# The head of a layer in a streaming encoder step: key latents projected last and normalised when their products are read out

## The chip, the cores and the metric

The kernel runs on one core of a Trainium2 chip. The metric is the device time of one execution in microseconds (us). Three timed runs of the kernel before took 2825.91, 2833.0 and 2838.61 us (median 2833.0). Two changed kernels that differ by less than about half a per cent (14 us) can hardly be told apart at that spread.

## The reference, cut to what matters

The program computes two layers for 576 tokens at once: 512 of a prompt and 64 of a sample that also sees 256 cached tokens. Each layer begins with one norm and one wide projection, of which the first three groups of columns concern us:

```python
u = rms_norm(x, g_pre_mix)                       # 576 x 1024
zq, zkv, zpe, ... = split_cols(u @ w_in)         # 384, 256, 32 columns, ...
q_a = rms_norm(zq, g_mla_q) @ w_mla_uq           # per head: 64 plain + 32 rotary columns
q_nope, q_pe = q_a[..., :64], rope(q_a[..., 64:], pos)
ckv = rms_norm(zkv, g_mla_kv)                    # key latents, also an output
kpe = rope(zpe, pos)                             # rotary key, shared by the heads, also an output
kv = concat([cache_ckv, ckv]) @ w_mla_ukv        # per head: 64 key + 64 value columns
o_a = softmax(q . k * scale, masked) @ v         # 8 heads
```

Then follow retention, band attention, the merge of the three branches, cross-attention and the MLP, and the same again in the second layer. Everything is float32.

## The kernel before, in words

All activations are held feature-major: 128 features lie on the partitions, 576 tokens along the free axis. Weights come as "units" of 128x1024; ACT starts the DMA of a unit, copies it into a rounded high part (`hi`), and POOL subtracts that from the raw unit to give the low part (`lo`, one instruction of 128x1024 on SBUF). A product is the sum of three matmuls (high by high, high by low, low by high), so an activation must be split in the same way before TensorE can take it.

A `project` is one "job": for kt tiles of 128 input features, 6 matmuls each (three products, two halves of 288 tokens), into one of two job buffers in PSUM. DVE reads each job out ("evicts" it) and so frees its buffer; TensorE waits in `slot()` until the buffer of the job before last is free. A job from the 1024-wide input has 48 matmuls; a job of one head from the key latents has 12, the one for the 256 cached tokens 6 (narrower), the query job 18.

An RMS norm's sum of squares is made by TensorE too: ACT squares a tile (`square`), and TensorE multiplies it with a matrix of ones (`stat`, 4 matmuls). ACT then takes the square root (`root_of`), and DVE the reciprocal (`invert`).

Order at the head of a layer (lines 431 to 436 on TensorE, 760 to 776 on ACT, 1094 to 1119 on DVE): the two jobs of the key latents (`CKV`), the job of the rotary key, two stats of the key latents, the three jobs of the query latents (`ZQ`). DVE evicts each job times the reciprocal of the input norm (`scale_job`), rotates the rotary key (1102 to 1106), inverts the key norm (1107), multiplies both key latents by gain and norm in place (1110), and splits key latents and cached latents in one piece of 1664 columns (1114). ACT rounds the three query latents and DVE makes their low parts (1119).

Then the first head begins (`steps_mla(0)` and the entry -1 of `PLAN_MLA`, where a plan says after which attention tile a step of the next head is issued, and -1 means ahead of the first): key/value job of the new tokens and of the cached ones, the three stats of the query latents, the query job, the transposition of the values (`turn_values`), and the two key/value jobs of the second head. DVE at that place evicts keys and values (1144 to 1148), inverts the query norm (1127), multiplies the rotary tables `COS` and `SIN` by it (1128, 1129), copies four rows of mask from `COS` into both query buffers (1131), and evicts the queries (1134 to 1139). Only then come the scores of the first tile. The query norm thus enters through the tables, and the key norm is already inside `CKV`. Each engine runs its own list in order, and all waits are on semaphores.

The lines that the change and the steps below touch:

```python
1110    v.scalar_tensor_tensor(out=CKV[:, k, 0:NT], in0=CKV[:, k, 0:NT], scalar=g_col("mla_kv", k),
1127    invert(rstd2[:, :])
1128    v.tensor_tensor(COS[0:QK, :], COS[0:QK, :], rstd2[0:QK, :], ALU.mult)
1129    v.tensor_tensor(SIN[QK:P, :], SIN[QK:P, :], rstd2[QK:P, :], ALU.mult)
1131    v.tensor_copy(Q[QK:QK + MASKS, c], COS[QK:QK + MASKS, :])
1145    free(v.tensor_copy(halves(vT[:, 0:NT]), job_halves(s)))
```

Of the kernel before, what the change touches and what calls it, by code (L numbers as in the profile page):

```python
# [13 lines left out]
P = 128  # L14
# [87 lines left out]
PLAN_MLA = plan(MLA_HEADS, NQ, (-1, 0, 2))  # L102
# [12 lines left out]
READY = 42  # L115
ROUNDS = 33
# [10 lines left out]
def build(nc, x_in, mem_in, w_in, ckv_in, kpe_in, state_in, bandk_in, bandv_in, memk_in, memv_in,  # L127
          bias_in, gain_in, gain_x_in, const_in, rope_in, mask_in, y_out, ckv_out, kpe_out, retp_out, rets_out,
          bandk_out, bandv_out, memk_out, memv_out):
    with ExitStack() as ctx:  # L130
# [42 lines left out]
        rstd_c = TMP[:, 1]  # L173
# [79 lines left out]
        def _(pe):  # L253
# [15 lines left out]
            with pe.Fori(0, DEPTH) as l:  # L269
# [45 lines left out]
                def project(s, kt, hl, at_col=0, step=P, m=P, pieces=HALVES, each_ready=0, stats=False,  # L315
                            each_evicted=False):
# [5 lines left out]
                    for k in range(kt):  # L322
                        if stats:
                            stat(k, kt)
                        if each_ready and k % each_ready == 0:
                            wait_ready()
# [104 lines left out]
                for i in range(CR + 1):  # L431
                    project(unit(), KT, U_HL, each_ready=int(i == 0))
                for k in range(CR):
                    stat(k, CR)
                for i in range(QR):
                    project(unit(), KT, U_HL)

                def steps_mla(h):
                    s = []

                    def keys_values():
                        if h == 0:
                            wait_ready()
                        s.append(unit())
                        project(s[0], CR, CKV_HL, at_col=QR * P)
                        project(s[0], CR, CKV_HL, at_col=QR * P, pieces=[(0, PAST, NT)])

                    def queries():
                        if h == 0:
                            for k in range(QR):  # L450
                                stat(k, QR)
                            wait_ready()
                        project(s[0], QR, ZQ_HL)

                    return [keys_values, queries,
                            lambda: turn_values(V_TOKENS + [(NT, P, 4), (NT + P, P, 5), (SEQ, DEC, 6)], but=1)]
# [147 lines left out]
        def _(act):  # L604
# [40 lines left out]
            with act.Fori(0, DEPTH) as l:  # L645
# [114 lines left out]
                for _ in range(CR + 1):  # L760
                    place()
                    n["job"] += 1
                for k in range(CR):
                    act.wait_ge(job_free, l * JOBS + k + 1 + 2)
                    square(k, CKV[:, k, 0:NT])
                root_of(rstd_c, CR * P)
                for _ in range(QR):
                    place()
                    n["job"] += 1
                evicted()  # L770
                for k in range(QR):
                    ins = round_hi(ZQ_HL[0][:, k], ZQ[:, k], "mla_q", k)
                ins.then_inc(rounded, 1)
                for k in range(QR):
                    square(k, ZQ[:, k])
                root_of(rstd2[:, :], QR * P)
# [8 lines left out]
                def steps_mla(h):  # L785
                    return [count(2, 1), count(1), count(1)]
# [103 lines left out]
        def _(dve):  # L890
# [19 lines left out]
            with dve.Fori(0, DEPTH) as l:  # L910
# [183 lines left out]
                for k in range(CR):  # L1094
                    scale_job(CKV[:, k, 0:NT])
# [11 lines left out]
                invert(rstd_c)  # L1107
                scale_job(ZQ[:, 1])
                for k in range(CR):
                    v.scalar_tensor_tensor(out=CKV[:, k, 0:NT], in0=CKV[:, k, 0:NT], scalar=g_col("mla_kv", k),  # L1110
                                           in1=rstd_c, op0=ALU.mult, op1=ALU.mult)
                dve.drain()
                z = Z0 + 2 * QR * NT
                is_ready(split(m_sb[:, QR * NT:QR * NT + CR * KEYS], arena[:, z:z + CR * KEYS],
                               arena[:, z + CR * KEYS:z + 2 * CR * KEYS]))
                scale_job(ZQ[:, 2])
                store()
                store()
# [578 lines left out]
```

## Time and profile before

| what | value |
|---|---|
| median of three timed runs | 2833.0 us |
| the profiled execution, its own time | 2829.17 us |
| its span in the trace | 2827.4 us |
| mean granted clock of TensorE | 0.959 of full |
| TensorE busy (matmul) | 2606.2 us, 92% |
| VectorE (DVE) busy | 1443.0 us, 51% |
| ScalarE (ACT) busy | 799.8 us, 28% |
| GpSimd (POOL) busy | 826.7 us, 29% |
| shares of the chain that ended last | PE 79%, DVE 10%, DVEq 6%, issue 2%, ACT 1% |

Busy times are sums over the whole span, and what bounds one stretch is seen only there. The chain that ended last goes back from the last instruction to what released it at each step; DVEq is the time in which DVE's own queue, its drains above all, passed from one instruction to the next. The granted clock is a share of TensorE's full 2.4 GHz; 0.5 is its lower level, 1.2 GHz. Where rows have a start time, it counts from the start of the span; the head of the first layer lies at 20 to 87 us, that of the second at 1411 to 1481 us, 1393.45 us later.

### The profile page before, as it was taken

To read this page: it belongs to the slowest core of one execution; us is meant where nothing else is said; L and a number is where in the kernel's file an instruction comes from. 1 tells how busy PE (TensorE), PEld (TensorE's weight loads), DVE (VectorE), ACT (ScalarE), POOL (GpSimd) and SP (SyncE) were. 2 spreads that over 40 slices of the span, in tenths; PEclk is the share of its full clock that TensorE was granted. 3 is DMA by queue.
4 is the path that set the end of the run, shared out by engine and by line. 5 is a ranking of instruction groups with operands and counts; after the bars stand their busy time and mean duration, and the time that the engine had idled before them with its cause. 6 is when DMAs were issued, how large, how long until landed. Compare 5 with 4: busy or idle time off the path is not lost.

```text
span 2827.4 us, 46601 instructions
## 1 busy us (share of the span) xinstructions
PE 2606.2 (92%) x17836; PEld 2395.7 (85%) x17836; DVE 1443.0 (51%) x2226; ACT 799.8 (28%) x1460; POOL 826.7 (29%) x335
## 2 busy tenths in 40 slices
PE   8789999999989799999788999899999898999996
PEld 7669888877988799999676798797779787999995
DVE  4661464354564755346756515624445648353366
ACT  4342112234324311111324421223343343111112
POOL 3113223211333234434221132132223232343342
PEclk9999999999999999999899999899999999999998
DMA  4102112221223122222221121121222221222222
GB/s 140 38 23 93 60 47 85 71 75 61 83 71 94 46 82 84 88 82 84 61 82 31 48 83 49 43 92 61 81 76 80 68 89 48 83 85 83 82 83 78
DMA packets 65687, 204.73 MB, mean 72 GB/s; under 512 B 7936, under 2 KB 16000, under 8 KB 65360
## 3 DMA queue, kind: packets, MB, share of 16 engines
q10 hardware_dynamic: 47808, 174.08, 20.1%
q1 hardware_dynamic: 17680, 27.90, 3.0%
q8 instruction: 136, 2.23, 0.3%
q14 instruction: 63, 0.52, 0.1%
HBM read 190.93 MB, written 11.03 MB: 71 GB/s over the span
## 4 chain that ended last, share of the span: by engine, by line
PE 79%; DVE 10%; DVEq 6%; issue 2%; ACT 1%; DMA 0%; SPq 0%; ACTq 0%
PE job L332 65%; PE outp L381 5%; PE scores L360 3%; DVE rstd L974 3%; PE turn L370 2%; DVEq L1001 2%; PE scores L262 1%; DVEq L1037 1%; PE job L341 1%; DVE arena L965 1%; DVE rstd L982 1%; PE job L350 1%; ACT probT L705 1%; DVE x L1002 1%; DVEq L980 0%
## 5 line engine op out<-in xcount | busy, mean ns | idle before, releaser
L332 PE MATMUL job<-arena,w_hi 128*128 128x288 f32 (+1 forms) x9984 | 1775.5, 300 | 46.5 <-DVE q L1139 16.7
L332 PEld LDWEIGHTS job<-arena,w_hi 128*128 128x128 f32 x9984 | 1494.3, 192 | 67.6 <-issue 22.3
L593 POOL TENSOR_TENSOR w_lo<-raw,w_hi 128x1024 fp32r<-128x1024 f32 x331 | 826.5, 2497 | 1968.7 <-ACT w_hi L612 1968.7
L332 PE MATMUL job<-arena,w_lo 128*128 128x288 f32 (+1 forms) x4992 | 1087.6, 297 | 0.0
L332 PEld LDWEIGHTS job<-arena,w_lo 128*128 128x128 f32 x4992 | 818.8, 191 | 0.0
L612 ACT ACTIVATE w_hi<-raw 128x1024 fp32r<-128x1024 f32 x331 | 349.6, 1056 | 1072.0 <-PE job L332 904.7
L381 PEld LDWEIGHTS outp<-probT,v 128*64 128x64 f32 (+2 forms) x992 | 111.4, 149 | 141.5 <-issue 71.3
L948 DVE TENSOR_TENSOR tmp<-job,rstd 128x576 f32<-128x576 f32 x70 | 53.0, 758 | 329.9 <-PE job L332 325.5
L381 PE MATMUL outp<-probT,v 128*64 128x128 f32 (+2 forms) x992 | 160.8, 291 | 51.4 <-DVE arena L1045 38.7
L262 PE MATMUL scores<-q,const 128*128 128x288 f32 (+1 forms) x296 | 99.0, 473 | 69.6 <-ACT q L673 60.6
L360 PE MATMUL scores<-k,q 128*128 128x256 f32 (+10 forms) x400 | 148.5, 455 | 13.1 <-DVE k L1341 4.4
L937 DVE CAST arena<-tmp 128x576 fp32r<-128x576 f32 x64 | 151.6, 2368 | 4.7
L716 ACT ACTIVATE arena<-outp 64x128 fp32r<-64x128 f32 (+3 forms) x200 | 52.4, 262 | 312.9 <-PE outp L381 312.5
L262 PEld LDWEIGHTS scores<-q,const 128*128 128x128 f32 x296 | 60.8, 222 | 92.1 <-ACT q L673 69.2
L1387 DVE TENSOR_TENSOR m<-job,m 128x576 f32<-128x576 f32 x48 | 36.4, 758 | 194.3 <-PE job L332 194.3
L747 ACT ACTIVATE tmp<-tmp,gain 128x576 f32<-128x576 f32 x48 | 37.3, 778 | 256.4 <-DVE tmp L948 256.4
L1376 DVE SCALAR_TENSOR_TENSOR tmp<-job,rstd 128x576 f32<-128x576 f32 x64 | 48.5, 758 | 110.4 <-PE job L332 110.1
L943 DVE COPY m<-job 128x576 f32<-128x576 f32 x48 | 36.3, 756 | 124.9 <-PE job L332 124.9
L370 PE MATMUL turn<-const,prob 128*128 128x128 f32 (+1 forms) x496 | 99.7, 300 | 0.0
L974 DVE RECIPROCAL rstd<-rstd 128x576 f32<-128x576 f32 x22 | 82.5, 3752 | 31.3 <-ACT rstd L626 27.4
L705 ACT ACTIVATE probT<-turn 128x256 f32<-128x256 f32 (+3 forms) x200 | 83.6, 418 | 36.4 <-PE turn L370 32.3
L1045 DVE TENSOR_TENSOR arena<-outp,arena 64x128 fp32r<-64x128 f32 (+3 forms) x200 | 55.0, 275 | 65.3 <-ACT arena L716 60.8
(145 smaller groups left out, 1718.1 us busy)
## 6 DMA issues: line engine op xcount, KB each, us to landing
raw<-in_w ACTq DMA_DIRECT2D x332, 512.0 KB, 3.6
bias<-in_bias SPq DMA_DIRECT2D x16, 256.0 KB, 3.4
x<-in_x SPq DMA_DIRECT2D x4, 576.0 KB, 8.7
cs<-in_rope SPq DMA_DIRECT2D x4, 576.0 KB, 4.6
out_o_bandk<-k SPq DMA_DIRECT2D x8, 288.0 KB, 4.0
out_o_bandv<-tmp SPq DMA_DIRECT2D x8, 288.0 KB, 5.0
out_y<-x SPq DMA_DIRECT2D x1, 2304.0 KB, 6.9
bias<-in_mem SPq DMA_DIRECT2D x8, 256.0 KB, 3.5
```

The lines of the kernel that those rows point to most:

```text
L262: mm = pe.matmul(scores_ps[:, po:po + nn], ONES, SQ[:, k % 2, so:so + nn], start=(k == 0), stop=(k == kt - 1))
L332: mm = pe.matmul(ps[0:m, po:po + nn], w[:, s, c:c + m], x[:, k, so:so + nn], start=(k == 0 and w is WHI and x is hl[0]), stop=(k == kt - 1 ...
L360: pe.matmul(score_ps[s][:, 0:w], Q[r0:r1, head["q"], t0:t0 + P], K[r0:r1, head["k"], c:c + w], start=True, stop=True).then_inc(score_done, 1)
L370: mm = pe.transpose(turn_ps[0:w, j * P:(j + 1) * P], PROB[:, it % 3, c:c + w], IDENT)
L381: mm = pe.matmul(out_ps[o0:o0 + v1 - v0, 0:P], V[0:w, head["vs"], t, v0:v1], probT[0:w, j * P:(j + 1) * P], start=(j == 0), stop=(j == len ...
L593: nc.gpsimd.tensor_tensor(WLO[:, u % RING, :], RAWS[:, u % RAW, :], WHI[:, u % RING, :].bitcast(F32), ALU.subtract).then_inc(lo_done, 1)
L612: act.activation(WHI[:, u % RING, :], RAWS[:, u % RAW, :], ACT.Copy).then_inc(hi_done, 1)
L705: ins = act.activation(probT[:, 0:full * P], turn_ps[:, 0:full * P], ACT.Copy)
L937: v.tensor_copy(hi, src)
L974: v.reciprocal(ap, ap)
L1001: dve.drain()
L1045: v.tensor_tensor(O_HL[1][o0:o1, ot, t0:t1], out_ps[o0:o1, c0:P], O_HL[0][o0:o1, ot, t0:t1].bitcast(F32), ALU.subtract).then_inc(out_free, 1)
```

## The change

Three things change in the head of each layer, and nothing else.

First, the order of the jobs: rotary key, three query latents, two key latents. The stats stand in the middle of the jobs (after four of the eight input tiles): those of the first two query latents inside the third query job, the third inside the first key job, that of the first key latent inside the second key job, and that of the second key latent ahead of the first query job. ACT rounds, squares and takes the root of each latent as it is evicted (`latent`). DVE now splits the cached latents alone (512 columns, between the evictions of the second and third query latent), makes the low parts of the queries, inverts the query norm and multiplies both tables, and then evicts the two key latents.

Second, the key norm. The key latents are multiplied by their gain alone on the way into the split (by ACT and DVE, as the query latents are). The reciprocal of the norm is multiplied where a head's key and value job is evicted: the two copies become multiplications by `rstd_c`, which now lies in `rstd2`, and it is inverted at the first head's eviction, behind the queries. The latents that are an output get gain and norm in place later, ahead of the value eviction of the second head (`store_latents`).

Third, the steps of a head: the first head runs cached keys and values, queries, new keys and values, and then its transposition, which waits for all evictions (`but=0`); the others run new, cached, queries, values. `PLAN_MLA` has four steps in place of three, the first two at the same tile.

```diff
-PLAN_MLA = plan(MLA_HEADS, NQ, (-1, 0, 2))
+PLAN_MLA = plan(MLA_HEADS, NQ, (-1, -1, 0, 2))
...
-rstd_c = TMP[:, 1]
+rstd_c = rstd2
...
             for k in range(kt):
                 if stats:
                     stat(k, kt)
+                if amid and k == kt // 2:
+                    amid()
                 if each_ready and k % each_ready == 0:
...
-        for i in range(CR + 1):
-            project(unit(), KT, U_HL, each_ready=int(i == 0))
-        for k in range(CR):
-            stat(k, CR)
-        for i in range(QR):
-            project(unit(), KT, U_HL)
+        def latent_stats(*which):
+            def add():
+                for k, kt in which:
+                    stat(k, kt)
+            return add
+        project(unit(), KT, U_HL, each_ready=1)
+        for after in (None, None, latent_stats((0, QR), (1, QR)), latent_stats((2, QR)), latent_stats((0, CR))):
+            project(unit(), KT, U_HL, amid=after)
         def steps_mla(h):
             s = []
-            def keys_values():
+            def weights():
+                if not s:
+                    s.append(unit())
+                return s[0]
+            def past():
                 if h == 0:
                     wait_ready()
-                s.append(unit())
-                project(s[0], CR, CKV_HL, at_col=QR * P)
-                project(s[0], CR, CKV_HL, at_col=QR * P, pieces=[(0, PAST, NT)])
+                project(weights(), CR, CKV_HL, at_col=QR * P, pieces=[(0, PAST, NT)])
             def queries():
                 if h == 0:
-                    for k in range(QR):
-                        stat(k, QR)
+                    stat(CR - 1, CR)
                     wait_ready()
-                project(s[0], QR, ZQ_HL)
-            return [keys_values, queries,
-                    lambda: turn_values(V_TOKENS + [(NT, P, 4), (NT + P, P, 5), (SEQ, DEC, 6)], but=1)]
+                project(weights(), QR, ZQ_HL)
+            def new():
+                if h == 0:
+                    wait_ready()
+                project(weights(), CR, CKV_HL, at_col=QR * P)
+            first = [past, queries, new] if h == 0 else [new, past, queries]
+            return first + [
...
-        for _ in range(CR + 1):
+        def latent(i):
+            act.wait_ge(job_free, l * JOBS + i + 2 + 2)
+            k, kt = (i, QR) if i < QR else (i - QR, CR)
+            src, hi_of, name = (ZQ[:, k], ZQ_HL[0][:, k], "mla_q") if i < QR else \
+                (CKV[:, k, 0:NT], CKV_HL[0][:, k, 0:NT], "mla_kv")
+            if i == 0:
+                act.wait_ge(layer_loaded, (l + 1) * 16 * LAYER_LOADS)
+            ins = round_hi(hi_of, src, name, k)
+            if k == kt - 1:
+                ins.then_inc(rounded, 1)
+            square(k, src)
+            if k == kt - 1:
+                root_of((rstd2 if i < QR else rstd_c)[:, :], kt * P)
+        for i in range(1 + QR + CR):
             place()
+            if i >= 2:
+                latent(i - 2)
             n["job"] += 1
-        for k in range(CR):
-            act.wait_ge(job_free, l * JOBS + k + 1 + 2)
-            square(k, CKV[:, k, 0:NT])
-        root_of(rstd_c, CR * P)
-        for _ in range(QR):
-            place()
-            n["job"] += 1
-        evicted()
-        for k in range(QR):
-            ins = round_hi(ZQ_HL[0][:, k], ZQ[:, k], "mla_q", k)
-        ins.then_inc(rounded, 1)
-        for k in range(QR):
-            square(k, ZQ[:, k])
-        root_of(rstd2[:, :], QR * P)
+        latent(QR + CR - 1)
...
-            return [count(2, 1), count(1), count(1)]
+            return [count(1, 1), count(1), count(1), count(1)]
...
-        for k in range(CR):
-            scale_job(CKV[:, k, 0:NT])
         scale_job(TMP[:, 0])
         scale_job(ZQ[:, 0])
@@ -1104,33 +1120,35 @@
         dve.drain()
         for b in range(2):
             v.tensor_tensor(K[NOPE:QK, b, 0:NT], TMP[NOPE:QK, 0], RTMP[NOPE:QK, :], ALU.add)
-        invert(rstd_c)
         scale_job(ZQ[:, 1])
+        is_ready(split(CKV[:, :, NT:KEYS], CKV_HL[0][:, :, NT:KEYS], CKV_HL[1][:, :, NT:KEYS]))
+        scale_job(ZQ[:, 2])
+        is_ready(lows(lambda k: ZQ[:, k], "mla_q", ZQ_HL, 0, QR))
+        invert(rstd2[:, :])
+        v.tensor_tensor(COS[0:QK, :], COS[0:QK, :], rstd2[0:QK, :], ALU.mult)
+        v.tensor_tensor(SIN[QK:P, :], SIN[QK:P, :], rstd2[QK:P, :], ALU.mult)
         for k in range(CR):
-            v.scalar_tensor_tensor(out=CKV[:, k, 0:NT], in0=CKV[:, k, 0:NT], scalar=g_col("mla_kv", k),
-                                   in1=rstd_c, op0=ALU.mult, op1=ALU.mult)
+            scale_job(CKV[:, k, 0:NT])
         dve.drain()
-        z = Z0 + 2 * QR * NT
-        is_ready(split(m_sb[:, QR * NT:QR * NT + CR * KEYS], arena[:, z:z + CR * KEYS],
-                       arena[:, z + CR * KEYS:z + 2 * CR * KEYS]))
-        scale_job(ZQ[:, 2])
-        store()
-        store()
-        is_ready(lows(lambda k: ZQ[:, k], "mla_q", ZQ_HL, 0, QR))
+        is_ready(lows(lambda k: CKV[:, k, 0:NT], "mla_kv", tuple(t[:, :, 0:NT] for t in CKV_HL), 0, CR))
+        def store_latents():
+            for k in range(CR):
+                v.scalar_tensor_tensor(out=CKV[:, k, 0:NT], in0=CKV[:, k, 0:NT], scalar=g_col("mla_kv", k),
+                                       in1=rstd_c[:, :], op0=ALU.mult, op1=ALU.mult)
+            store()
+            store()
         def steps_mla(h):
             b = h % 2
             def queries():
+                s = job()
                 if h == 0:
-                    invert(rstd2[:, :])
-                    v.tensor_tensor(COS[0:QK, :], COS[0:QK, :], rstd2[0:QK, :], ALU.mult)
-                    v.tensor_tensor(SIN[QK:P, :], SIN[QK:P, :], rstd2[QK:P, :], ALU.mult)
                     for c in range(2):
                         v.tensor_copy(Q[QK:QK + MASKS, c], COS[QK:QK + MASKS, :])
-                    dve.drain()
-                s = job()
                 v.scalar_tensor_tensor(out=halves(Q[0:QK, b]), in0=job_halves(s, 0, QK), scalar=QK ** -0.5,
                                        in1=halves(COS[0:QK, :]), op0=ALU.mult, op1=ALU.mult)
                 v.scalar_tensor_tensor(out=halves(RTMP[NOPE:QK, :]), in0=job_halves(s, QK, P), scalar=QK ** -0.5,
@@ -1138,22 +1156,31 @@
                 dve.drain()
                 free(v.tensor_tensor(Q[NOPE:QK, b], Q[NOPE:QK, b], RTMP[NOPE:QK, :], ALU.add))
-            def keys_values():
+            def new_keys_values():
                 s = job()
-                v.tensor_copy(halves(K[0:NOPE, b, 0:NT]), job_halves(s, 0, NOPE))
-                free(v.tensor_copy(halves(vT[:, 0:NT]), job_halves(s)))
+                if h == 0:
+                    invert(rstd_c[:, :])
+                v.tensor_tensor(halves(K[0:NOPE, b, 0:NT]), job_halves(s, 0, NOPE), halves(rstd_c[0:NOPE, :]),
+                                ALU.mult)
+                free(v.tensor_tensor(halves(vT[:, 0:NT]), job_halves(s), halves(rstd_c[:, :]), ALU.mult))
+            def past_keys_values():
                 s = job()
                 v.tensor_copy(K[0:NOPE, b, NT:KEYS], job_ps[s][0:NOPE, 0:PAST])
                 free(v.tensor_copy(vT[:, NT:KEYS], job_ps[s][:, 0:PAST]))
             def values():
+                if h == 1:
+                    store_latents()
                 s = job()
                 v.tensor_copy(V[:, b, 0:4, 0:MLA_V], tiles(job_ps[s][:, 0:512], 4)[:, :, NOPE:P])
                 v.tensor_copy(V[:, b, 4:6, 0:MLA_V], tiles(job_ps[s][:, 512:768], 2)[:, :, NOPE:P])
                 free(v.tensor_copy(V[0:DEC, b, 6, 0:MLA_V], job_ps[s][0:DEC, 768 + NOPE:768 + P]))
-            return [keys_values, queries, values]
+            steps = [new_keys_values, past_keys_values, queries, values]
+            return [steps[i] for i in (1, 2, 0, 3)] if h == 0 else steps
...
-for i in range(CR):
-    add(cols(zkv + i * P))
 pe_w = w[:, zpe:zpe + ROPE]
 add(w_tile(np.concatenate([np.zeros((D, NOPE), np.float32), pe_w, swapped(pe_w)], 1)))
 for i in range(QR):
     add(cols(zq + i * P))
+for i in range(CR):
+    add(cols(zkv + i * P))
```

## Rows read from the trace of the kernel before

**Rows 1.** Windows: stretch, length; busy PE, PEld, DVE, ACT, POOL; granted clock; DMA.

```profile
1422.00:1454.00 32.00, 32.00 (x235) 31.46 (x233) 13.75 (x12) 6.02 (x7) 11.74 (x5) 1.00 0.26 81
1454.00:1476.00 22.00, 10.96 (x58) 9.63 (x58) 18.29 (x21) 7.96 (x10) 4.86 (x2) 0.82 0.25 79
82.00:98.00 16.00, 13.12 (x61) 10.53 (x61) 8.72 (x22) 3.87 (x13) 0.00 (x0) 0.78 0.00 0
```

**Rows 2.** Timeline by start, second layer: TensorE's first instructions after its gaps.

```profile
1456.76 0.79 PE L332 MATMUL job<-arena,w_hi 128*128 128x288 f32 x4 [2.65 <-DVE arena L939]
1475.42 1.33 PE L332 MATMUL job<-arena,w_hi 128*128 128x288 f32 x4 [8.38 <-DVE q L1139]
1480.80 0.92 PE L360 MATMUL scores<-k,q 100*128 100x128 f32 x4 [1.53 <-DVE tmp L1148]
```

**Rows 3.** Timeline, first layer: the first scores.

```profile
86.79 0.92 PE L360 MATMUL scores<-k,q 100*128 100x128 f32 x4 [1.00 <-DVE tmp L1148]
```

**Rows 4.** Chain that ended last, second layer: start, length, piece.

```profile
1464.69 3.75 DVE rstd L974
```

**Rows 5.** Timeline, second layer, while the projections run.

```profile
1426.63 0.76 DVE L948 TENSOR_TENSOR m<-job,rstd 128x576 f32<-128x576 f32 x1 [5.64 <-PE job L332]
1427.59 1.24 ACT L673 ACTIVATE q<-m 128x576 f32<-128x576 f32 x2
1427.77 2.41 POOL L593 TENSOR_TENSOR w_lo<-raw,w_hi 128x1024 fp32r<-128x1024 f32 x1 [3.93 <-ACT w_hi L612]
1432.83 2.10 PE L262 MATMUL scores<-q,const 128*128 128x288 f32 x8
1434.55 0.91 PE L332 MATMUL job<-arena,w_hi 128*128 128x288 f32 x4
```

**Rows 6.** Timeline, second layer: POOL beside DVE on SBUF.

```profile
1468.53 0.75 DVE L1128 TENSOR_TENSOR cs<-cs,rstd 96x576 f32<-96x576 f32 x1
1468.97 2.51 POOL L593 TENSOR_TENSOR w_lo<-raw,w_hi 128x1024 fp32r<-128x1024 f32 x1 [0.95 <-ACT w_hi L612]
1469.30 2.80 DVE L1129 TENSOR_TENSOR cs<-cs,rstd 32x576 f32<-32x576 f32 x1
```

**Rows 7.** Forms of lines 937, 1131: ns min/median/max, first and last start.

```profile
L937 DVE CAST arena<-tmp x64: 459/2495/2499, 988.6 to 2735.6; 128x576 fp32r<-128x576 f32 x64
L1131 DVE COPY q<-cs x4: 449/449/450, 77.9 to 1472.4; 4x576 f32<-4x576 f32 x4
```

**Rows 8.** Timeline, second layer: rounding, stats and queries of the first head.

```profile
1457.21 2.11 ACT L629 ACTIVATE arena<-m,gain 128x576 fp32r<-128x576 f32 x3 [8.32 <-DVE m L948]
1463.50 0.91 PE L332 MATMUL job<-arena,w_hi 128*128 128x288 f32 x4
1463.91 0.74 ACT L626 ACTIVATE rstd<-scores,const 128x576 f32<-128x576 f32 x1 [1.33 <-PE scores L262]
1465.67 2.35 POOL L593 TENSOR_TENSOR w_lo<-raw,w_hi 128x1024 fp32r<-128x1024 f32 x1 [14.32 <-ACT w_hi L612]
1466.11 0.93 PE L350 MATMUL job<-const,tmp 128*128 128x128 f32 x7
1473.01 0.76 DVE L1134 SCALAR_TENSOR_TENSOR q<-job,cs 96x576 f32<-96x576 f32 x1 [0.17 <-issue]
1478.59 0.75 DVE L1144 COPY k<-job 64x576 f32<-64x576 f32 x1 [2.45 <-PE job L332]
```

**Rows 9.** A window behind the second layer's first gap.

```profile
1458.00:1462.00 4.00, 4.00 (x17) 3.56 (x17) 2.65 (x4) 2.57 (x5) 0.00 (x0) 0.60 0.48 168
```

**Rows 10.** Costliest groups: the weights' high part on ACT: busy, mean ns, idle.

```profile
L612 ACT ACTIVATE w_hi<-raw 128x1024 fp32r<-128x1024 f32 x331 | 349.6, 1056 | 1072.0 <-PE job L332 904.7
```

**Rows 11.** Form of line 1110; timeline at the second head's values, first layer.

```profile
L1110 DVE SCALAR_TENSOR_TENSOR m<-m,gain,tmp x4: 810/812/815, 58.5 to 1452.6; 128x576 f32<-128x576 f32 x4
...
99.89 0.28 DVE L1045 TENSOR_TENSOR arena<-outp,arena 64x128 fp32r<-64x128 f32 x1 [0.38 <-ACT arena L716]
100.83 1.09 PE L381 MATMUL outp<-probT,v 128*64 128x128 f32 x8 [0.25 <-ACT probT L705]
```

More of the change, by code:

```diff
@@ L114 @@
 REQS = 3 * KT + RET_HEADS + RET_HEADS // 2
-READY = 42
-ROUNDS = 33
+READY = 43
+ROUNDS = 34
 ROOTS = 9 + RET_HEADS
@@ L315, in project @@
                 def project(s, kt, hl, at_col=0, step=P, m=P, pieces=HALVES, each_ready=0, stats=False,
-                            each_evicted=False):
+                            each_evicted=False, amid=None):
                     ps = slot()
@@ L458, in _ @@
+                    return first + [
+                            lambda: turn_values(V_TOKENS + [(NT, P, 4), (NT + P, P, 5), (SEQ, DEC, 6)], but=min(h, 1))]
                 heads = [dict(q=h % 2, k=h % 2, rows=(0, QK + MASKS), tiles=Q_TILES, vs=h % 2,
```

## The prediction

> **What bounds the kernel now.** I read the stages by windows first. While the projections of a layer's head run, TensorE is busy for 32.00 of 32 us at full clock; right behind them it is busy for only 10.96 of 22 us and DVE for 18.29 [rows 1]. So only that short stretch, once a layer, can change much. The timeline shows its gaps: 2.65 us until DVE has split the key latents, 8.38 us until it has evicted the first queries, and 1.53 us until the evictions ahead of the first scores [rows 2]. In the first layer the first scores start at 86.79, which is 1480.24 on the second layer's time [rows 3]; in the second at 1480.80 [rows 2]. The chain that ended last runs through the query norm's reciprocal, 3.75 us from 1464.69 [rows 4]. What counts is thus when DVE is through with the evictions that the first scores need, not TensorE's busy share.
>
> **Up to the fifth job.** I work on the second layer's time; the first layer has the same steps. The third job has been issued at 1432.83 and a job takes 6.40 us (evictions of 0.76 with 5.64 of waiting for TensorE between them); two stats take 1.72, until 1434.55 [rows 5]. The new order moves no matmul off TensorE: the same six jobs and five stats run. The fourth job, with two stats inside, ends at 1432.83 + 6.40 + 1.72 = 1440.95; ACT has squared the first two latents by about 1435.5, before they are wanted at 1436.03. The fifth, with one stat, ends at 1448.21. The split of the cached latents (512 of 1664 columns) and the rotation of the key lie on DVE between evictions 6.40 us apart and cost nothing; without that cover the split costs under the 2.65 us that the whole one shows [rows 2].
>
> **The sixth job, a new wait.** It wants the square of the first key latent at its middle, 1448.21 + 3.20 = 1451.41. DVE evicts that latent only behind the query norm and both tables. The third query latent is evicted by 1441.9; ACT first rounds a weight unit, 1.06 us from about 1441.1 [rows 10], then the latent, until 1442.9; then DVE makes three low parts. POOL starts 1.34 us behind a job's issue end (1427.77, the job before the eviction at 1426.63 having ended at 1426.43) and runs 2.4 us [rows 5]. The product of two SBUF tiles on 32 partitions that starts 0.33 us after POOL takes 2.80 us and ends 0.62 after POOL does, where its neighbour took 0.75 [rows 6]. So the first low part waits for POOL until 1444.6, all three are done at about 1446.75, the reciprocal of 3.75 [rows 4] at 1450.5; then the table product meets POOL's next unit (1449.55 to 1451.95) and ends at 1452.55, the second table at 1453.2, the eviction at 1454.05. ACT starts 0.2 behind it, rounds in 0.70 (three in 2.11 [rows 8]) and squares in 0.7: stat at 1455.65. TensorE waits 4.25 us. Bounds: 2.5 if neither meeting happens; 6.4 if POOL's weight unit comes late and holds the second table too. I take 4.25, since both meetings follow from job ends. The job's end is then 1455.65 + 0.86 + 3.20 = 1459.7; before, all six were through at 1434.55 + 3 x 6.40 = 1453.75.
>
> **From there to the first scores.** Eviction of the second key latent to 1460.65, ACT as above, last stat at 1462.25, issued by 1463.1 (call it S). The cached keys' job fits in between. Queries 2.61 us (1463.50 to 1466.11 [rows 8]), visible to DVE at S + 2.8. ACT's root starts at S + 0.41 and POOL's next unit at S + 2.17, as before (1463.50, 1463.91, 1465.67 [rows 8]), so POOL is 0.6 us ahead of the two mask copies. Alone such a copy takes 0.449 us; a cast of SBUF to SBUF takes 0.459 alone and 2.495 in most of its 64 runs [rows 7]. No row shows the copy beside POOL, so its bounds are 0.82 us for both and S + 2.17 + 2.35 + 0.75 = S + 5.3 for their end; I take the latter, since the cast is the nearest row. Query eviction 2.4 (1473.01 [rows 8] to 1475.42, where TensorE is released [rows 2]) with a drain: S + 7.85. Now the key norm's reciprocal, 3.75, which nothing covers: S + 11.75. Two products of 0.76 out of PSUM, 1.5: S + 13.3 = 1476.4. TensorE waits for this with the transposition (`but=0`), behind which the second head's two jobs stand: a gap of about 9 us, in place of the 8.38. Before, from the queries' release (1475.42) to the first scores it took 5.38 [rows 2]; now the transposition, 0.95, stands ahead of the same two jobs: 1476.4 + 0.95 + 5.38 = 1482.75. Bounds: 1.4 less if those jobs run at full clock (4 matmuls from 1475.42 took 1.33, 0.91 at most elsewhere [rows 2, 5]; twelve at 6.40 us per 48 are 1.6, and DVE's first eviction, now at 1478.59 [rows 8], comes 1.4 earlier), 1.0 more if the transposition too runs at half clock.
>
> Against before: 1482.75 - 1480.80 = +1.95 in the second layer and 1482.75 - 1480.24 = +2.5 in the first. **Head: +4.45.** The two removed gaps come back as two others.
>
> The Trainium skill, SBUF — State Buffer, section Who interferes with whom, says that an fp32 copy from SBUF to SBUF takes the port pair that DVE shares with GpSimd and is blocked for a whole GpSimd instruction. By it the copies wait as I have them; without it the copies end at S + 3.6, and the sum would be 3.4 us lower in all, 2834.1. No run here shows this form beside POOL; the cast of rows 7 agrees with the page.
>
> **Gain and norm of the stored latents.** They leave the path at the head, where they took two instructions of 0.812 us, and stand ahead of the second head's value eviction [rows 11]. Behind that on DVE are the maxima of the sixth tile and the release of an output, which ends at 100.17 now and at 101.8 then; TensorE's next weighting starts at 100.83 and needs it [rows 11]. So about 0.95 of the 1.65 us comes through per layer, bounds 0 and 1.8 (a drain more): **+1.9.** The two output DMAs asked for behind it start later on SP, which has nothing else to issue until the eight heads are done, and only there DVE waits for them.
>
> **Evictions of keys and values.** Copies of 0.75 us [rows 8] become products of 0.76 [rows 5] out of PSUM: two in each of 16 heads, 0.3 us if none is hidden, nothing where TensorE is the bound. I take 0. The plan's fourth step changes no order beyond the first head.
>
> **The clock.** TensorE's clock fell to 0.60 in the 4 us behind a gap of 2.65 us [rows 9]; the new gap of 4.25 stands inside a job whose second half, 3.20 us, is all on the path. At half clock for that half: +3.2; not at all: 0. I take 1.0 a layer, nearer to none, as only a part of the half need lie in such a stretch: **+2.0.**
>
> **Sum.** 4.45 + 1.9 + 2.0 = +8.35 us: 2829.17 + 8.35 = 2837.5. The profiled execution lies 3.8 us under the median of the timed runs (2833.0) and inside their spread; I state 2838, a little on the median's side of the sum.
>
> **Rivals.** (1) The meetings with POOL don't happen and the clock holds: the sixth job waits 1.75 less, the copies cost 1.7 less, the jobs at the end 1.4 less, and 1.0 of clock falls away: -5.85 a layer, 2837.5 - 11.7 = 2826. For it: the meetings hang on half microseconds. Against it: POOL's starts are tied to the same job ends as DVE's work.
> (2) The change wins what it takes away: the query norm is off the path and nothing takes its place, both gaps of 2.65 and 8.38 go: -22, 2807. For it: the query norm now has two jobs beside it. Against it: the key norm's reciprocal stands in the same place of DVE's list.
> (3) Slower: the clock. With gaps of 4.25, about 2 and 9 us within 27 us, TensorE stays at 1.2 GHz from the sixth job's middle well into the first head. Price a layer: second half +3.2, last stat and queries +3.5, transposition +1, and in the attention +2 (82 to 98 us had a mean of 0.78 in the first layer [rows 1]), less the 1.0 counted: +8.7, 2837.5 + 17.4 = 2855. It decides from a clock at 0.5 throughout 1455 to 1466. Against it: even behind the gap of 8.38 us that mean is well over 0.5, so the clock comes back soon after work does.
>
> **How the numbers follow.** Forecast 0.68, rival 1 0.15, rival 2 0.06, rival 3 0.11. Under 0.5% (14 us) a run cannot be told from no change; forecast and rival 1 lie within that, though 0.01 of the forecast's end is slower: faster 0.06, same 0.82, slower 0.12. The bounds give, per layer, -5.85 and -0.95 (stores hidden) against +2.1 (a longer sixth wait), +2.2 (clock), +0.85 and +1: 2824 to 2850. That leaves out rivals 2 and 3, 0.17.
>
> **What would show it.** In the changed trace: TensorE's wait inside the sixth job for ACT's square, 2.5 to 6; the table product lengthened by POOL; mask copies of over 2 us; the reciprocal behind the query eviction with TensorE idle for 7 to 10 us ahead of the transposition; first scores 1 to 4 us later from the head's start than before. I am wrong if DVE evicts the first key latent before 1452, or if the gap ahead of the transposition is under 5 us.

## The result, and the profile after

The changed kernel takes 2840.59 us (median of 20 runs, 2820.70 to 2845.62), the kernel before 2830.48 beside it (20 runs, 2812.15 to 2839.36). The ratio is 1.0035 with an interval of 1.002 to 1.005: slower, by 5.7 to 14.2 us; the middle of that, 9.9, lies under the half per cent (14 us) that was taken as hard to tell from no change. The forecast was 2838, its sum +8.35. The ratio of the version with both mends, further down, leaves out one execution of 2944.83 us, whose mean granted clock was 0.83 where the others had 0.96.

One measure serves for all that follows. "Head" is the time from the start of DVE's eviction of the third job to the start of the first scores; first layer, then second:

| kernel | head, us | against before |
|---|---|---|
| before | 47.21, 47.77 | |
| after | 51.88, 52.03 | +4.67, +4.26 |

The evictions at which it starts in the second layer, before and after; the first scores are in [rows 2], [rows 3] and further down:

```profile
1433.03 0.76 DVE L948 TENSOR_TENSOR tmp<-job,rstd 128x576 f32<-128x576 f32 x1 [5.64 <-PE job L332]
...
1437.21 0.76 DVE L966 TENSOR_TENSOR m<-job,rstd 128x576 f32<-128x576 f32 x1 [0.43 <-PE job L334]
```

The windows of the second layer in the changed kernel (stretch, length; busy PE, PEld, DVE, ACT, POOL; granted clock; DMA share and GB/s) answer to [rows 1]:

```profile
1422.00:1454.00 32.00, 32.00 (x232) 31.37 (x232) 15.80 (x14) 9.76 (x12) 10.38 (x4) 1.00 0.24 78
1456.00:1460.00 4.00, 0.04 (x1) 0.00 (x0) 2.61 (x3) 1.33 (x2) 0.48 (x1) 0.83 0.02 9
1460.00:1465.00 5.00, 4.93 (x16) 4.36 (x17) 0.00 (x0) 0.02 (x1) 0.00 (x0) 0.50 0.00 0
1465.00:1468.00 3.00, 2.69 (x19) 2.48 (x18) 0.76 (x1) 0.19 (x1) 0.00 (x0) 0.92 0.00 0
1483.00:1486.00 3.00, 2.90 (x13) 2.87 (x14) 0.74 (x3) 1.03 (x1) 0.00 (x0) 0.51 0.00 0
```

While the projections run, nothing differs for TensorE. Then it stands still for 4 us; it starts again at 0.50, which is 1.2 of 2.4 GHz, and has its full clock back only after 1465. The timeline names the wait (start, length, engine, line; in brackets the idle time before and what ended it):

```profile
1447.29 3.85 DVE L983 SCALAR_TENSOR_TENSOR arena<-m,gain,arena 128x576 fp32r<-128x576 f32 x3 [1.00 <-ACT arena L643]
1451.06 3.74 DVE L992 RECIPROCAL rstd<-rstd 128x576 f32<-128x576 f32 x1
1454.11 2.37 POOL L607 TENSOR_TENSOR w_lo<-raw,w_hi 128x1024 fp32r<-128x1024 f32 x1 [5.04 <-ACT w_hi L626]
1454.87 2.22 DVE L1128 TENSOR_TENSOR cs<-cs,rstd 96x576 f32<-96x576 f32 x1
1457.88 0.76 DVE L966 TENSOR_TENSOR m<-job,rstd 128x576 f32<-128x576 f32 x1
1460.07 2.29 PE L262 MATMUL scores<-q,const 128*128 128x288 f32 x4 [4.02 <-ACT q L687]
1461.74 1.57 PE L334 MATMUL job<-arena,w_hi 128*128 128x288 f32 x4
1466.82 0.40 PE L334 MATMUL job<-arena,w_hi 128*128 128x256 f32 x2
...
1472.25 2.38 POOL L607 TENSOR_TENSOR w_lo<-raw,w_hi 128x1024 fp32r<-128x1024 f32 x1 [15.77 <-ACT w_hi L626]
1472.86 2.46 DVE L1151 COPY q<-cs 4x576 f32<-4x576 f32 x2 [2.04 <-PE job L334]
1477.73 3.75 DVE L992 RECIPROCAL rstd<-rstd 128x576 f32<-128x576 f32 x1
1483.10 1.75 PE L352 MATMUL job<-const,tmp 128*128 128x128 f32 x7 [8.67 <-DVE tmp L1166]
1484.50 1.31 PE L334 MATMUL job<-arena,w_hi 128*128 128x288 f32 x4
1489.24 0.92 PE L362 MATMUL scores<-k,q 100*128 100x128 f32 x4 [1.54 <-DVE tmp L1172]
```

Read down DVE: low parts (L983), the query norm's reciprocal (L992), a table product (L1128) that ends behind POOL, and only then the eviction of the first key latent (L966), whose square TensorE awaits inside the sixth job: 4.02 us. A second such chain ends in 8.67 us of waiting ahead of the transposition: mask copies (L1151) that end behind POOL, the queries' evictions, and the key norm's reciprocal, uncovered. The gaps of 2.65 and 8.38 us [rows 2] are gone, and these stand in their place. A smaller wait, 1.51 us, stands ahead of the last stat. The first layer has the same two long ones, 4.02 and 8.68.

The stored latents, first layer, at the second head's values:

```profile
101.56 0.62 PE L383 MATMUL outp<-probT,v 128*64 128x128 f32 x4 [1.44 <-DVE arena L1063]
103.35 1.54 DVE L1138 SCALAR_TENSOR_TENSOR m<-m,gain,rstd 128x576 f32<-128x576 f32 x2
106.04 0.27 DVE L1063 TENSOR_TENSOR arena<-outp,arena 64x128 fp32r<-64x128 f32 x1
106.46 1.06 PE L383 MATMUL outp<-probT,v 128*64 128x128 f32 x8 [0.99 <-DVE arena L1063]
```

From the weighting of four matmuls to that of eight it now takes 106.46 - 101.56 = 4.90 us, 4.16 before. The release of an output (L1063) ends the wait, as [rows 11] let expect.

The sum of the traces is 4.67 + 4.26 + 2 x 0.75 = +10.4 us, inside the measured 5.7 to 14.2. The two profiled executions themselves differ by 3.2 us of span, so about 7 us the other way lie outside these places, 6.0 of them behind the second layer's first scores; single executions of one kernel differ by more than that (2812.15 to 2839.36 before), and I did not trace the cause.

### The profile page after: what moved, and what is told of

It reads as the page before. It is cut to its first block, busy times and chain, and to the rows that moved or that the text cites. A ratio compares the mean times of both kernels' runs of the same rounds, so it can differ in the third digit from the quotient of the medians.

```text
span 2830.6 us, 46613 instructions
## 1 busy us (share of the span) xinstructions
PE 2605.2 (92%) x17836; PEld 2393.1 (85%) x17836; DVE 1447.0 (51%) x2230; ACT 802.9 (28%) x1464; POOL 827.7 (29%) x335
## 4 chain that ended last, share of the span: by engine, by line
PE 79%; DVE 10%; DVEq 6%; issue 3%; ACT 1%; DMA 0%; ACTq 0%; SPq 0%
PE job L334 65%; PE outp L383 4%; PE scores L362 3%; DVE rstd L992 2%; PE turn L372 2%; DVEq L1019 2%; PE scores L262 2%; DVEq L1055 1%; DVE arena L983 1%; PE job L343 1%; DVEq L993 1%; DVE rstd L1000 1%; PE job L352 1%; ACT probT L719 1%; DVE x L1020 1%
## 5 line engine op out<-in xcount | busy, mean ns | idle before, releaser
L966 DVE TENSOR_TENSOR tmp<-job,rstd 128x576 f32<-128x576 f32 x70 | 53.1, 758 | 330.8 <-PE job L334 326.1
L992 DVE RECIPROCAL rstd<-rstd 128x576 f32<-128x576 f32 x24 | 90.0, 3750 | 29.8 <-ACT rstd L640 25.9
L362 PEld LDWEIGHTS scores<-k,q 100*128 100x128 f32 (+2 forms) x400 | 61.7, 192 | 29.8 <-issue 14.9
```

The lines of the kernel that those rows point to most:

```text
L362: pe.matmul(score_ps[s][:, 0:w], Q[r0:r1, head["q"], t0:t0 + P], K[r0:r1, head["k"], c:c + w], start=True, stop=True).then_inc(score_done, 1)
L966: free(v.tensor_tensor(halves(dst), job_halves(s), halves(rstd[:, :]), ALU.mult))
L992: v.reciprocal(ap, ap)
```

## The experiments

Theory: the change loses by its two new waits, the first with a low clock behind it. Each edit is on the changed kernel, save where said; where the verdict is a single run, it rests on the trace.

**Both key stats behind the sixth job.** The order of all else stays.

```diff
-latent_stats((2, QR)), latent_stats((0, CR))):
+latent_stats((2, QR)), None):
     ...
-stat(CR - 1, CR)
+for k in range(CR): stat(k, CR)
```

> The stat of the first key latent no longer stands inside the sixth job but with the other one, ahead of the first query job. I call 'head' the time from the start of the third job's eviction to the start of the first scores: 47.21 and 47.77 us in the two layers before, 51.88 and 52.03 after. Theory (the wait inside the sixth job holds back the eviction of the second key latent, and all that follows): the sixth job ends about 6 us earlier (4.0 us of wait, 0.9 to 1.9 us of low clock, 0.86 of stat), the last stat is issued 6 to 7.5 us earlier, the head falls to 44.5 to 46 us, and the whole kernel comes out at 0.996 to 1.000 of the time before. Rival (DVE's list sets the end, and TensorE's wait only moves to the stats ahead of the queries): the head falls by less than 2 us and the ratio stays at 1.002 to 1.005.

Heads 45.04 and 45.04; ratio to before 0.9988 (0.9965 to 1.0011, 12 runs). The first layer:

```profile
61.89 0.76 DVE L967 TENSOR_TENSOR m<-job,rstd 128x576 f32<-128x576 f32 x1 [0.64 <-PE job L334]
62.69 1.24 PE L262 MATMUL scores<-q,const 128*128 128x288 f32 x4
64.08 1.24 PE L262 MATMUL scores<-q,const 128*128 128x288 f32 x4 [0.16 <-ACT q L688]
64.94 0.90 PE L334 MATMUL job<-arena,w_hi 128*128 128x288 f32 x4
84.85 0.92 PE L362 MATMUL scores<-k,q 100*128 100x128 f32 x4 [1.41 <-DVE tmp L1173]
```

TensorE finishes the sixth job while DVE catches up, and both stats follow with 0.16 us of waiting, where the changed kernel waits 1.51 ahead of the last one. The place of one stat cost the changed kernel 6.8 to 7.0 us a layer; that alone turns its loss into no measurable difference.

**The key norm's reciprocal ahead of the query eviction**, where DVE waits for the queries' job anyway.

```diff
 def queries():
+    if h == 0: invert(rstd_c[:, :])
     s = job()
     ...
 def new_keys_values():
-    if h == 0: invert(rstd_c[:, :])
```

> The reciprocal of the key norm stands ahead of the first queries' eviction on DVE, where DVE waited 2.04 us for the query job, and no longer behind it. Theory (the reciprocal of 3.75 us is uncovered, and the mask copies are slow because POOL holds the port): the reciprocal runs from about 0.1 us behind ACT's root, the copies then come behind POOL's unit and take 0.8 us for both in place of 2.46, and the first head's key and value eviction ends 3.1 us earlier: heads of 48.8 and 48.9 us, ratio about 1.0013. Rival (the copies are slow by themselves, on 4 partitions behind a table product): they stay at 2.4 us and the heads fall by 1.5 us only, to 50.4 and 50.5.

Heads 48.52 and 48.71; ratio 1.0011 (0.999 to 1.0031). The first layer:

```profile
72.58 3.75 DVE L992 RECIPROCAL rstd<-rstd 128x576 f32<-128x576 f32 x1 [0.44 <-ACT rstd L640]
73.57 2.39 POOL L607 TENSOR_TENSOR w_lo<-raw,w_hi 128x1024 fp32r<-128x1024 f32 x1 [14.69 <-ACT w_hi L626]
76.48 0.83 DVE L1153 COPY q<-cs 4x576 f32<-4x576 f32 x2 [0.15 <-issue]
81.25 1.75 PE L352 MATMUL job<-const,tmp 128*128 128x128 f32 x7 [5.51 <-DVE tmp L1166]
```

The reciprocal lies over POOL's instruction and keeps its 3.75 us; the copies behind it take 0.83. The gap falls by 3.17 us.

**POOL's weight unit placed later** in the first head, nothing else moved.

```diff
-[count(1, 1), count(1), count(1), count(1)]
+[count(1, int(h > 0)), count(1), count(1), count(1, int(h == 0))]
```

> ACT rounds the weight unit of the first head one job later, behind the first head's new keys, so that POOL's low part does not run beside the first queries' eviction; nothing else is changed. Theory (POOL's instruction blocks the two mask copies): the copies take 0.8 us for both in place of 2.46, and the heads fall by 1.65 us to 50.2 and 50.4. Rival (they are slow for another reason): still 2.4 us, the heads as after, 51.9 and 52.0.

Heads 49.55 and 49.91, one run of 2835.98 us.

```profile
74.64 0.83 DVE L1151 COPY q<-cs 4x576 f32<-4x576 f32 x2 [2.04 <-PE job L334]
77.38 2.67 POOL L607 TENSOR_TENSOR w_lo<-raw,w_hi 128x1024 fp32r<-128x1024 f32 x1 [18.10 <-ACT w_hi L626]
```

With POOL at 77.38 instead of 73.91 the same copies take 0.83 us in place of 2.47. That is 1.64 us; the head gained 2.33 and 2.12, 0.5 to 0.65 more than expected. In the first layer 0.57 of that lies behind the new keys' eviction (6.44 us to the first scores, 7.01 in the changed kernel), in the same instructions at another clock. In the second, the stat and the rest of the sixth job took 0.90 less than in the changed kernel and the way behind the new keys' eviction 0.38 more (6.65 us for 6.27).

**Stored latents without their norm.** It leaves out the two products of `store_latents`, so the stored latents lack gain and norm.

```diff
 def store_latents():
-    for k in range(CR):
-        v.scalar_tensor_tensor(out=CKV[:, k, 0:NT], ...)
```

> Leaves out the two multiplications of the stored key latents by gain and norm ahead of the second head's value eviction (the latents given out are not normalised then); the two output DMAs stay. Theory (about half of the 1.6 us comes through): from the first scores to the fourth weighting with 8 matmuls it takes 14.0 us, as before, in place of 14.8, the heads themselves are unchanged, and nothing of the whole time can be told. Rival (wholly hidden): 14.8 still.

One run of 2844.31 us, which says nothing at this size. The measure I had named, from the first scores on, holds differences of clock too (14.04 and 12.49 us in the two layers of before), so it failed. Between the two weightings it is plain:

```profile
100.36 0.62 PE L383 MATMUL outp<-probT,v 128*64 128x128 f32 x4 [1.44 <-DVE arena L1063]
104.52 1.09 PE L383 MATMUL outp<-probT,v 128*64 128x128 f32 x8 [0.25 <-ACT probT L719]
```

4.16 us, as before, and the wait is ACT's 0.25 again [rows 11]. So the store costs 4.90 - 4.16 = 0.74 us in this layer; from the first scores to the same weighting the changed kernel takes 0.78 and 0.75 longer than the one before in the two layers.

**Matmuls on constants in the sixth job's gap**, to tell the low clock from the wait.

```diff
 def add():
+    if which == ((0, CR),):
+        for _ in range(4):
+            pe.matmul(turn_ps[:, 0:512], ONES, const[:, 0:512], ...)
```

> Four matmuls of constants (128x512, some 0.85 us each, into a bank that nothing else uses there) stand in the sixth job ahead of the wait for the stat, so that TensorE works through most of the 4.0 us gap. Theory (the second half of the sixth job ran longer, 4.2 and 5.1 us in place of 3.2, because the granted clock fell behind the gap): it takes 3.2 us in both layers, and the heads fall by 1.0 and 1.9 us, to about 50.9 and 50.1. Rival (the longer half has another cause, such as weights or reads that come late): it stays at 4.2 to 5.1 and the heads don't fall.

Heads 50.30 and 50.00, one run of 2839.63 us. The first layer; the columns of the window further down are as above:

```profile
57.83 3.59 PE L438 MATMUL turn<-const 128*128 128x512 f32 x8
62.02 1.24 PE L262 MATMUL scores<-q,const 128*128 128x288 f32 x4 [0.59 <-ACT q L690]
62.88 0.90 PE L334 MATMUL job<-arena,w_hi 128*128 128x288 f32 x4
66.28 0.40 PE L334 MATMUL job<-arena,w_hi 128*128 128x256 f32 x2
```

The half job in the second layer:

```profile
1470.50 0.89 PE L334 MATMUL job<-arena,w_hi 128*128 128x288 f32 x4
...
1473.89 0.40 PE L334 MATMUL job<-arena,w_hi 128*128 128x256 f32 x2
```

The window behind the gap, first layer:

```profile
62.00:66.00 4.00, 3.98 (x26) 3.77 (x27) 0.00 (x0) 0.00 (x0) 0.00 (x0) 1.00 0.02 4
```

The four constants (eight records) end 0.59 us ahead of the square, which comes no earlier for them; behind it the clock is 1.00. The stat takes 62.88 - 62.02 = 0.86 us instead of 1.67, and the second half of the job, to the first matmul of 256 columns, 66.28 - 62.88 = 3.40 (1473.89 - 1470.50 = 3.39 in the second layer) instead of 4.18 (first) and 1466.82 - 1461.74 = 5.08 (second). The low clock cost 0.81 + 0.78 = 1.6 us here in the first layer and 0.81 + 1.69 = 2.5 in the second. The heads fell by 1.58 and 2.03; in the second layer 0.46 went into a slower way behind the new keys' eviction (6.73 us for 6.27).

**Both mends together**, the first two edits in one kernel.

> Both mends together: the stat of the first key latent out of the sixth job, and the reciprocal of the key norm ahead of the first queries' eviction. Theory (two waits in a row on one path, so their prices add): heads of 45.04 - 3.3 = 41.7 us in both layers (47.21 and 47.77 before), ratio to before about 0.9965. Rival (with the first wait gone, the reciprocal is covered by something else that is then late, the query job or POOL's unit): heads of 43.5 to 45 us, ratio 0.998.

Heads 41.80 and 41.87; median 2819.01 us of five runs, ratio 0.9936 (0.9911 to 0.9961).

```profile
65.96 3.75 DVE L993 RECIPROCAL rstd<-rstd 128x576 f32<-128x576 f32 x1 [0.44 <-ACT rstd L641]
69.86 0.83 DVE L1154 COPY q<-cs 4x576 f32<-4x576 f32 x2
74.63 1.75 PE L352 MATMUL job<-const,tmp 128*128 128x128 f32 x7 [5.52 <-DVE tmp L1167]
81.44 0.92 PE L362 MATMUL scores<-k,q 100*128 100x128 f32 x4 [1.54 <-DVE tmp L1173]
```

The two waits were independent: the single gains would give 51.88 - 6.84 - 3.36 = 41.68 in the first layer. TensorE still waits 5.52 us ahead of the transposition.

**New keys ahead of the queries**, on top of the first mend, with the reciprocal at the new keys' eviction.

```diff
-first = [past, queries, new] if h == 0 else [new, past, queries]
+first = [past, new, queries] if h == 0 else [new, past, queries]
     ...
-turn_values(..., but=min(h, 1))
+turn_values(..., but=1)
```

> As the first mend, and the first head runs cached, new, queries, values: the two stats, the key and value job and its eviction with the reciprocal stand ahead of the queries, so that the transposition runs while DVE evicts the queries (it waits for all but the last eviction). Theory (the transposition and its gap were on the path only behind the queries): heads of 39 to 40.5 us, ratio about 0.995, better than both kernels. Rival (the first scores need the queries too, and DVE has the same list to work off, so the order inside the list is worth little against the reciprocal moved forward alone): heads of 41.5 us, as with both mends.

Heads 41.34 and 43.43; ratio 0.9951 (0.9932 to 0.997). The heads missed the theory's 39 to 40.5, though the ratio came out as it said: the first layer is where its rival put it, the second 1.6 us above both mends. The second layer:

```profile
1470.57 0.96 PE L352 MATMUL job<-const,tmp 128*128 128x128 f32 x7 [3.13 <-DVE tmp L1166]
1472.78 2.34 POOL L607 TENSOR_TENSOR w_lo<-raw,w_hi 128x1024 fp32r<-128x1024 f32 x1 [5.23 <-ACT w_hi L626]
1472.90 2.83 DVE L1157 TENSOR_TENSOR q<-q,bias 32x576 f32<-32x576 f32 x1
1475.78 1.33 PE L334 MATMUL job<-arena,w_hi 128*128 128x288 f32 x4 [4.25 <-DVE q L1157]
```

The transposition still waits 3.13 us for the eviction of the values (5.52 with both mends), and behind it the next head's key job waits again, 1.41 us in the first layer and 4.25 in the second, since it needs the buffer that only the query eviction frees. The earlier transposition also lets ACT and POOL start the next weight unit sooner, and in the second layer it meets that eviction's last add: 2.83 us in place of 0.75. In the first layer the add started 0.65 us ahead of POOL and kept 0.75.

**Constants in both gaps** (the edit above, and nine such matmuls ahead of the transposition).

> As the run with constants in the sixth job, and nine more such matmuls, some 7.7 us, behind the first head's key job, in the gap of 8.7 us ahead of the transposition. Theory (clock): the transposition takes 0.93 us in place of 1.40 from its start to the next job's, the twelve matmuls behind it 1.6 in place of 2.3 to 3.0, and the heads fall to 48.5 to 49.5 us. Rival (the evictions on DVE set the end there whatever the clock): under 0.7 us less than the run with the first filling alone.

Heads 48.24 and 48.25, one run of 2833.65 us: 2.06 and 1.75 us less than with the first gap alone filled, where the rival allowed 0.7. The transposition runs at full clock, 0.98 us against 1.75:

```profile
82.58 0.98 PE L352 MATMUL job<-const,tmp 128*128 128x128 f32 x7 [0.96 <-DVE tmp L1172]
87.40 0.92 PE L362 MATMUL scores<-k,q 100*128 100x128 f32 x4 [1.53 <-DVE tmp L1178]
```

**Both mends and six constants in the gap that they leave.**

```diff
 def new():
     ...
+    if h == 0:
+        for _ in range(6):
+            pe.matmul(turn_ps[:, 0:512], ONES, const[:, 0:512], ...)
```

> Both mends, and six matmuls of constants (some 5.1 us) behind the first head's key job, in the gap of 5.5 us that is left ahead of the transposition. Theory (the clock that falls in that gap costs the transposition 0.45 us and the second head's jobs 1.3, and the first items of the attention run slow behind it): heads of 39.8 to 40.2 us in place of 41.8, and some 2 us more inside the first head, ratio to before 0.990 to 0.993. Rival (the evictions on DVE follow at their own pace): heads of 41.3 us or more, ratio as with both mends alone (0.9936).

Heads 39.83 and 39.81; median 2816.22 us, ratio 0.9928 (0.9906 to 0.9951). This version beats the kernel before, and so do the two mends without the constants; the times of these two cannot be told apart, their heads can:

```profile
74.18 0.98 PE L352 MATMUL job<-const,tmp 128*128 128x128 f32 x7 [0.36 <-DVE tmp L1170]
79.00 0.92 PE L362 MATMUL scores<-k,q 100*128 100x128 f32 x4 [1.53 <-DVE tmp L1176]
```

The further 2 us expected inside the first head came in the first layer alone: from the first scores to the weighting of four matmuls it takes 8.33 us in place of 11.11 with the two mends, at a clock of 1.00 in place of 0.69. In the second layer it takes 9.90 and 9.91.

**Constants in the kernel before**, nine in its gap of 8.38 us.

```diff
 def values():
     turn_values(..., but=1)
+    if h == 0:
+        for _ in range(9):
+            pe.matmul(turn_ps[:, 0:512], ONES, const[:, 0:512], ...)
```

> The kernel before, with nine matmuls of constants (some 7.7 us) behind the first transposition, in its gap of 8.38 us. It tells how much of what the filling brings does not belong to the change at all. Theory (clock): heads of 45.8 and 46.3 us in place of 47.21 and 47.77, ratio 0.998 to 0.999. Rival: no change of the heads beyond 0.3 us.

Heads 45.82 and 46.20; ratio 0.9971 (0.995 to 0.9991).

```profile
80.90 0.79 PE L332 MATMUL job<-arena,w_hi 128*128 128x288 f32 x4 [0.59 <-DVE q L1144]
85.01 0.92 PE L360 MATMUL scores<-k,q 100*128 100x128 f32 x4 [1.53 <-DVE tmp L1153]
```

The matmuls that took 1.33 us behind the gap [rows 2] take 0.79, and from the first scores to the weighting of four the first layer takes 8.33 us in place of 9.88. So with the long gaps filled in both orders (the gap of 2.65 us of the kernel before was left as it is) the unmended new one still loses (48.24 against 45.82) and the mended one wins (39.83).

Heads (with 1.5 us for the stores, where the version has them) and timed runs agree for the changed kernel (+10.4 us by the traces, +9.9 by the ratio), for the late stats (-4.9 + 1.5 = -3.4, and -3.4) and for the early reciprocal (+3.8, +3.1). The other four timed versions were faster than their heads say: both mends -9.8 against -18.1, the new keys first -8.7 against -13.9, both mends with constants -13.8 against -20.4, the constants in the kernel before -3.0 against -8.2. For the second and the fourth the interval still holds the sum of the heads; for the two mended versions the upper ends stand at -11.1 and -13.9. By the medians these two gain 16.4 and 16.6 us. The stretch behind the first scores does not explain it: with both mends it is longer (11.11 and 9.91 us to the weighting of four) than in the kernel before (9.88 and 8.33). What else they may gain was not traced and stays open.

## Why the prediction was right, point by point

- **Up to the fifth job**: right. No gap there, and the projections stay at full clock.
- **The sixth job's wait**: 4.02 us for 4.25. Both meetings with POOL came: the low parts took 3.85 us for three, the table product 2.22. The eviction started at 1457.88; set back by the 4.18 us by which this execution's third eviction is later than before's, that is 1453.70, and its end 1454.46 for the 1454.05 worked out. The wait was shorter, but the stat did not come earlier: it started 22.86 us behind the third eviction in both layers, for 22.62. TensorE reached its place 0.46 us late, as a job and two stats take 8.32 us from eviction to eviction in both kernels (1433.03 to 1441.35 before), not 6.40 + 1.72.
- **The clock behind it**: the term that was mis-sized. I took 1.0 us a layer. Against the run with the gap filled (0.86 us for the stat, 3.40 and 3.39 for the half job) the stat lost 0.81 in both layers and the half job 0.78 and 1.69: 1.6 and 2.5 us. I had argued that only part of the half job need lie in the slow stretch and had left out the stat ahead of it. Even at full clock the half job takes 0.2 more than the 3.20 of the sum. The rival of a low clock throughout did not come: it returned within 3 to 5 us of work.
- **Mask copies and reciprocal**: 2.46 us and 3.75, as chosen. The run with POOL's unit later shows that the copies waited for POOL. The rule drawn on in the prediction (the Trainium skill, SBUF — State Buffer, section Who interferes with whom) is borne out by the trace: 0.83 us without a POOL instruction beside the copies, 2.46 with one.
- **The gap ahead of the transposition**: 8.67 us for about 9. From the sixth job's end to the end of the new keys' eviction it took 16.15 us in both layers for 16.7. From the end of the new keys' eviction to the first scores: 7.01 and 6.27 us for 6.33. The transposition ran at half clock, 1.75 against 0.98, which was a named bound.
- **The stored latents**: 0.75 us a layer for 0.95.
- **Evictions of keys and values at nothing**: nothing in the heads asks for a price; not tested alone.
- **The signs named**: the wait, the table product, the mask copies and the gap of 7 to 10 us came as said. The first scores came 4.67 and 4.26 us later, not 1 to 4; with the 1.0 us of clock that was counted they would have come 3.5 and 3.0 later.

Head and clock were forecast at 4.45 + 2.0 = 6.45 and measured 8.93: of the 2.5 more the clock makes 2.1 (4.1 less 2.0), the half jobs at full clock 0.4, the later stats 0.5 and the way behind the new keys' eviction 0.6; the way up to it takes off 1.1. With the stores 8.35 became 10.4. That 2838 lies so near to 2840.59 is in part luck: these errors cancel in part, and the forecast's base, one execution of 2829.17, happened to lie near the later median of 2830.48. Of the rivals, the one in which the meetings don't happen and the one in which both gaps simply go are refuted by the timeline. What the prediction didn't see is how cheaply the waits could be avoided: both came from the place of one instruction in an engine's order.

## What to carry to other kernels

When a stall is moved, follow the releasing engine's list to the next consumer: here the query norm left the path, and the key norm and the squares took its place at nearly the same price. Put a reduction's matmul where its input is ready, even if that is a job later, and a long operation where its engine waits anyway; these two moves took 10 us off the head of each layer, and the reordering without them lost 4 to 5. Whether such moves would gain as much in the old order was not tried. Count the clock behind every new gap of TensorE, the first instructions included.

## What was not expected of the hardware

- Copies of only four partitions wait for POOL's instruction to end: two that started 0.6 us into it ended 0.7 behind its end and took 2.46 us, 0.83 without it; the reciprocal, which reads one tile, kept 3.75 us beside POOL.
- The gap of 4.02 us was followed by a clock of 0.50 for up to 5 us of full work. Matmuls whose result nobody reads kept it at 1.00, and since they stood in a wait the heads show no price for them: they took off 1.4 to 2.1 us of head for each gap filled, in the kernel before, in the changed one's sixth job or in the mended one.
